# Input differences inside the delta rule's last steps, the gate weights read first, and a set of transposes spread over three steps

## What is computed

```python
h = rms_norm(x, norm_pre[i])
(aq, ak, av, az, dq, dk, dv, db, da, dz, gate_att, gate_dn) = split_cols(h @ w_in[i])
...
o_dn = bidir_gated_deltanet(qd, kd, vd, g, beta).astype(x.dtype)
o_dn = rms_norm(o_dn.transpose(0, 2, 1, 3), dn_norm[i]).reshape(B, S, DN_VW)
y_dn = (o_dn * jax.nn.silu(dz)) @ w_br_dn[i]
mix = (jax.nn.sigmoid(gate_att) * y_att + jax.nn.sigmoid(gate_dn) * y_dn) @ w_out[i]
```

```python
v_new = u_c - jnp.einsum('bhcd,bhdv->bhcv', w_c, state)
o = (jnp.einsum('bhcd,bhdv->bhcv', q_c * jnp.exp(g_c)[..., None], state)
     + jnp.einsum('bhcj,bhjv->bhcv', a_c, v_new))
k_dec = k_c * jnp.exp(g_last[..., None] - g_c)[..., None]
state = state * jnp.exp(g_last)[..., None, None] + jnp.einsum('bhcd,bhcv->bhdv', k_dec, v_new)
```

## Time and profile before

| what | value |
|---|---|
| median of 3 runs | 1669.21 us (1666.99 to 1671.65) |
| profiled execution, its own time | 1670.91 us |
| profiled execution, span in the trace | 1669.1 us |
| granted TensorE clock, mean | 0.959 |
| PE busy | 1478.6 us, 89% |
| DVE busy | 675.9 us, 40% |
| ACT busy | 380.5 us, 23% |
| POOL busy | 296.7 us, 18% |

### The profile page before, as it was taken

One profiled execution on the slowest core, in us unless ns is written; L12 is line 12 of the kernel. 1 busy time (PEld: TensorE's weight loads), 2 busy tenths in 40 slices (PEclk: granted clock), 3 DMA queues, 4 the chain that ended last, 5 costly groups with the idle time before them and its releaser, 6 DMA issues. The chain is left out here.

```text
span 1669.1 us, 22426 instructions
## 1 busy us (share of the span) xinstructions
PE 1478.6 (89%) x8686; PEld 995.7 (60%) x8686; DVE 675.9 (40%) x1203; ACT 380.5 (23%) x814; POOL 296.7 (18%) x261
## 2 busy tenths in 40 slices
PE   5998998999999978988999999999988968887782
PEld 5864445884544457777888778674657854332320
DVE  3321435124369956775232154310363444332224
ACT  3213445104333333321110132301231010000001
POOL 0020011620007244563540000000000002111110
PEclk9999999999999979999999999999988978999996
DMA  6128210213112213434322030322133066999994
GB/s 208 49 81 261 68 51 26 84 43 126 51 51 76 64 64 126 130 131 136 101 86 92 1 126 26 78 64 79 38 93 127 1 241 238 422 425 425 424 388 170
DMA packets 118385, 228.27 MB, mean 137 GB/s; under 512 B 13202, under 2 KB 102896, under 8 KB 109332
## 3 DMA queue, kind: packets, MB, share of 16 engines
q1 hardware_dynamic: 112963, 216.34, 36.0%
q0 software_dynamic: 5184, 8.55, 1.4%
q10 hardware_dynamic: 144, 2.10, 0.3%
HBM read 221.56 MB, written 15.74 MB: 142 GB/s over the span
## 5 line engine op out<-in xcount | busy, mean ns | idle before, releaser
L917 PE MATMUL psv<-arena 128*128 128x256 f32 x800 | 175.8, 379 | 2.7 <-ACT arena L1681 1.3
L882 PE MATMUL psv<-arena,wslot 128*128 128x512 f32 x384 | 170.8, 598 | 1.8 <-DVEq L2154 1.8
L917 PEld LDWEIGHTS psv<-arena 128*128 128x128 f32 x800 | 151.6, 190 | 25.3 <-issue 4.9
L1586 ACT ACTIVATE arena<-pss 128x512 f32<-128x512 f32 (+1 forms) x157 | 84.8, 540 | 333.1 <-PE pss L882 275.2
L882 PE MATMUL pss<-wslot,arena 128*128 128x256 f32 (+1 forms) x640 | 147.6, 391 | 4.6 <-issue 2.0
L882 PE MATMUL pss<-arena 128*128 128x256 f32 (+1 forms) x512 | 141.7, 434 | 6.3 <-ACTq L151 3.1
L1504 PE MATMUL pss<-arena 128*64 128x512 f32 x384 | 123.9, 655 | 18.8 <-DMA arena<-w_expert_in 16.4
L882 PEld LDWEIGHTS pss<-wslot,arena 128*128 128x128 f32 x640 | 120.7, 190 | 30.3 <-issue 11.8
L882 PEld LDWEIGHTS pss<-arena 128*128 128x128 f32 x512 | 95.9, 190 | 45.6 <-issue 29.8
L882 PEld LDWEIGHTS psv<-arena,wslot 128*128 128x128 f32 x384 | 71.1, 190 | 85.5 <-issue 83.0
L2364 DVE SCALAR_TENSOR_TENSOR arena<-psv,ccols,arena 128x510 f32<-128x510 f32 (+1 forms) x96 | 71.9, 749 | 59.9 <-ACT arena L1737 56.8
(11 more groups left out here) (339 smaller groups left out, 1977.6 us busy)
## 6 DMA issues: line engine op xcount, KB each, us to landing
arena<-w_expert_in SPq DMA_DIRECT2D x24, 2048.0 KB, 18.3
wslot<-w_in SPq DMA_DIRECT2D x32, 1024.0 KB, 5.4
arena<-w_expert_out SPq DMA_DIRECT2D x32, 1024.0 KB, 18.8
wslot<-w_ada SPq DMA_DIRECT2D x18, 1024.0 KB, 5.2
wslot<-w_expert_in SPq DMA_DIRECT2D x8, 2048.0 KB, 16.0
arena<-w_in SPq DMA_DIRECT2D x10, 1024.0 KB, 8.7
arena<-w_ada SPq DMA_DIRECT2D x6, 1024.0 KB, 7.9
arena<-x SPq DMA_DIRECT2D x8, 512.0 KB, 8.6
```

The source lines that it names most:

```text
L882: m = mm(o, l, r, start=(n == 0), stop=(n == len(pairs) - 1))
L917: m = mm(o[:, j * HALF_T:(j + 1) * HALF_T], l[:, c, j * P:(j + 1) * P], r[:, c, :], start=new and j == 0 and c == 0, stop=j == 1 and c == ...
L1586: L.did(A(dst, src, func, **kw), s[sig] if sig else None, [s["free_s"]])
```

## The change

Four edits are made together.

1. POOL makes the input differences `terms(hT, term_z, n)` for the `dz` and `gd` products behind its work in loop passes n = 4 (one), 5 (two) and 6 (one) of the delta rule, where before they followed `phase(3)`. They lie in the parts of `vtok` that are no longer read.
2. `last_part(4)` also moves ahead of `phase(3)`. Its output has a place of its own (`part_z`), and the held parts `held_b` move.
3. SP issues `dz` 2 and 3 first after `phase(3)`, then `gd` 0 and 1, and only then the parked `mixT`; norm rows, x, p and ctx follow between later weights, since `pin` and `ctxt` now share memory with the differences.
4. The transposes for g = 1 are spread: one half in step 0, two in step 1, one and the multiply in step 2, each ahead of the state update. `turn_back` has an argument for the halves.

```diff
@@ SP
             sp.wait_ge(s["phase"], 4 * 3)
+            stream_to(("gd", 1))
             load(mixT.rearrange("p c n -> p (c n)"), mix_dram.rearrange("(p n) -> p n", p=P), "mix_kept")
+            stream_to(("gd", 3))
             load(rowv, a["norm_post"].partition_broadcast(P), "ld_res")
             load(rowv2, a["ple_norm"].partition_broadcast(P), "ld_res")
             for t in range(NT):
                 load(x1[:, t, :], a["x"][0, t * P:(t + 1) * P, :], "ld_res")
+            stream_to(("brd", 1))
+
+            sp.wait_ge(s["full_v"], SEVEN_JOB[4] + 2)
             load(pin, a["p"][0, 0].rearrange("(t p) n -> p t n", p=P), "ld_p")
+            stream_to(("brd", 3))
+
+            sp.wait_ge(s["full_v"], SEVEN_JOB[8])
@@ POOL
+                if n == 4:
+                    terms(hT, term_z, 0)
+                if n == 5:
+                    terms(hT, term_z, 1)
+                    terms(hT, term_z, 2)
+                if n == 6:
+                    terms(hT, term_z, 3)
+            parts(4, part_z)
+            last_part(4, part_z)
             phase(3)
-            for n in range(3):
-                terms(hT, term_z, n)
-            last_part(4, part_b)
-            terms(hT, term_z, 3)
             for u in range(5, 7):
                 parts(u, part_b)
                 last_part(u, part_b)
@@ DVE
                 if n == 0:
                     dve.wait_ge(s["bsub_ready"], 1)
-                    turn_back(1, True)
+                    turn_back(1, True, (0,))
+                if n == 1:
+                    turn_back(1, True, (1,))
+                    turn_back(1, False, (0,))
+                if n == 2:
+                    turn_back(1, False, (1,))
+                    L.raise_(s["bt_ready"])
...
-                if n == 1:
-                    turn_back(1, False)
-                    L.raise_(s["bt_ready"])
```

More of the change, by code:

```diff
@@ L321, in build @@
         part_b = [at(tt_at, 4, WC), at(tt_at + 4 * K, 4, WC), at(B + 108 * K, 4, WC)]
[L322 to L325, removed]
+        part_z = part_b[0:2] + [at(B + 48 * K, 4, WC)]
+        held_b = [at(B + 96 * K + n * SEQ, 2, HALF_T) for n in range(4)]
+        term_z = [at(B + 60 * K, 4, HALF_T), at(B + 56 * K, 4, HALF_T), hT[:, 0:4, HALF_T:SEQ],
+                  at(B + 52 * K, 4, HALF_T)]
         term_n = [at(B + 64 * K, 4, HALF_T), at(B + 68 * K, 4, HALF_T), onT[:, 0:4, HALF_T:SEQ],
@@ L1228, in _ @@
             phase(3)
-            seven(4, hT, part_b, term_z, True)
+            seven(4, hT, part_z, term_z, True)
             for t in range(NT):
@@ L2069, in _ @@
                         keys(n + 1, hg)
-            parts(4, part_b)
+                if n == 4:
[7 more added lines that the diff above has]
+            last_part(4, part_z)
             phase(3)
-            for n in range(3):
-                terms(hT, term_z, n)
-            last_part(4, part_b)
-            terms(hT, term_z, 3)
             for u in range(5, 7):
@@ L2310, in inverse_norms, with turn_back @@
                     scale(o, o, c1, s["rk_in"])
-            def turn_back(g, first):
-                for x in range(2):
+            def turn_back(g, first, halves=(0, 1)):
+                for x in halves:
                     X = inv_X[HX[x], g, :, :]
@@ L2318, in turn_back @@
                                       X.rearrange("p r c -> p c r") if flip else X))
-                if not first:
+                if not first and 1 in halves:
                     mul(TTb[:, g], TT32[:, g], spread(co_b[:, g * 32:(g + 1) * 32], 32))
```

## The result

The changed kernel is slower: median 1678.13 us (1675.46 to 1679.69, 5 executions) against 1670.4 for the kernel before (5 executions on the same chip), a ratio of 1.0056 with the interval 1.0045 to 1.0068. A second comparison gave 1.0057 (1.0040 to 1.0074). One execution of a later kernel, `e6_last_part_behind`, took 3926.6 us and is left out of its ratio. The forecast was 1671, no change that can be told, with a range up to 1676: both are wrong.

The account below looks back on a forecast made before the run. PE, busy 89%, was taken to bound the kernel. Terms -4.3 + 1.0 + 4.8 + 0 = +1.5 us on the profiled 1670.91 give 1672.4; with the median 1.7 lower, the forecast was 1671, range 1663.5 to 1676.

Parts of the forecast that it names:

- Transposes: Delta rule steps 1 and 2: without DVE's transposes and multiply between them, step 2 shortens; -4.3 us, bounds -4.7 and -1.0.
- Differences in the steps: Passes 4 to 6: PE waits 2.5 to 2.9 us for POOL's key decay, costing 0.2 to 1.4 us.
- The last part ahead of phase(3): POOL's last part reaches DVE's last output additions, one of which may wait: 0 to 1 us on arrival at T, `phase(3)`.
- Behind phase(3): `seven(4)`: POOL's `parts(5)` and last part collide with DVE's four multiplies, delaying PE's last half; +4.8 us, bounds -2.1 and +4.8.
- The clock: Last half of `seven(4)`: low clock behind the wait both before and after; 0 more, bounds -1.7 and +3.7 us.
- rival 2: Last half of `seven(4)` and transposes behind it: 8 us wait holds PE at 1.2 GHz, +3.7, total 1674.4 us; chance 0.16.
- Reordered transfers: Behind `phase(3)`: `mixT`, x, p and ctx come later but are used only from `seven(8)`, over 80 us on; 0 us.
- The sum: Whole kernel: -4.3 + 1.0 + 4.8 + 0 = +1.5 us on the profiled execution, forecast median 1671.
- Rival 1: Behind `phase(3)`: DVE's multiplies don't collide with POOL; 1662 us, or 1664 if the clock still falls; chance 0.19.

Follow-up runs that it names:

- e6_last_part_behind: Changed kernel with `parts(5)` held until DVE's multiplies are done, one difference per pass 3 to 6, last part behind `phase(3)`: 1664.89 us, 0.9966; again 1663.71, 0.9974.
- after_again: The changed kernel itself, run a second time: 1679.58 us, ratio 1.0057 to the kernel before.
- e7: Changed kernel with only the last part of `seven(4)` moved back behind `phase(3)`: 1673.4 us, ratio 1.0030 to the kernel before.
- p1: Changed kernel with 2 repeated matmuls (0.9 us) ahead of the first product with `w_out`: ratio 1.0057 to the kernel before.
- p2: Changed kernel with 4 repeated matmuls (1.7 us) ahead of the first product with `w_out`: ratio 1.0068 to the kernel before.
- p3: Kernel before with 6 repeated matmuls (2.6 us) ahead of the first product with `w_out`: ratio 1.0013 to the kernel before.
- e1: Kernel before with the spread transposes alone: 1665.21 us, ratio 0.9972; again 1666.2 us, 0.9981.
- e5: Kernel before with only the new order of transfers (`dz` 2 and 3 and `gd` ahead of `mixT`, x, p, ctx): 1673.59 us, ratio 1.0029.
- e2: Changed kernel with POOL's `parts(5)` held until DVE's four multiplies are done: 1667.65 us, ratio 0.9994 to the kernel before.

## Why the prediction was wrong

**Transposes: right.** Steps 1 and 2 together are 3.9 us shorter in the trace (+0.30 and -4.24), forecast 4.3; alone they are worth 3 to 5 us.

**Differences in the steps: the wait right, its cost too high.** 2.62 us on PE as forecast. `phase(3)` is 4.4 us earlier, forecast 3.3. From step 6's start to step 7's new values the change costs 0.3 us (21.13 against 20.81), at the low end of the forecast's 0.2 to 1.4; the wait before the new values shrank so far that they kept their clock, 2.0 us that I had not counted (from them to the inner output 4.27 against 6.30). In after_again they did not keep it (3.44 us behind 3.17 us of waiting). A slip without effect: the forecast's terms for the key decay add up to 715.9 to 716.2, not to 716.2 to 716.6.

**The last part ahead of phase(3): the first step that failed.** "One of which may wait for POOL, 0 to 1 us." The addition did wait, 1.2 us. But I priced only the arrival at T, and not that PE's wait ahead of T grows from 1.75 to 2.94 us, behind which the next half runs at low clock for a while (+1.5). I had the rows for that: 2.12 us had been enough before the last half. The term was 0 to 1 us and is 2.7 in the trace; by the ratios of e7 and e6 it is 2.5 to 4.7.

**Behind phase(3): mechanism right, the clock missing from the term.** Forecast +4.8, measured +6.9 (43.01 - 36.12). The last half begins at T+31.35, forecast 30.4: 1.5 of that is the slow first half, and without it, in e7, it is T+29.86. So the collision itself costs 4.2 us (29.86 - 25.66), a little less than forecast, and the low clock 1.5 in the first half and 1.2 in the last. The multiplies take 11.22 us, forecast "some 11".

**The clock: the second step that failed.** "I take 0 more, bounds -1.7 and +3.7." The last half takes 6.57 us, 1.2 more than before, behind 7.83 us of waiting. This is rival 2's mechanism at a third of its price. Summed over the execution the low clock accounts for more than these 2.7 us (mean 0.957 against 0.961). The sum had no term for what lies behind `seven(5)`, and 3 to 7 of the 9.4 us are there: at 775 us the two traces of the changed kernel are 2.5 and 6.3 us behind (3.3 of the 6.3 already at the start of step 2). Over four traces each (p1, p2 and p3 count too, since their added work comes later) the changed kernel reaches `seven(5)` at 775.5 us on the mean and the kernel before at 772.4, which leaves some 6 of the 9.4 us behind it. Reckoned so for the others (their traces for the start of `seven(5)`, their ratios for the total), every kernel built on the changed one loses 2 to 6 us behind it, and those built on the kernel before (e1, e5, p3) lie between a gain of 1.4 and a loss of 3.1. That points at something which all of the first have, moved buffers among it, but one trace against a median is a rough measure, and no run takes it apart. The traces put this rest behind 1160 us, at waits that every kernel has; why the changed kernel pays more there on the mean stays open.

The Trainium skill, "SBUF — State Buffer", section "Who interferes with whom", has it that a DVE instruction with two SBUF inputs and a GpSimd instruction that reads SBUF exclude each other. The multiplies agree, with a small second input too: 2.0 to 2.1 us for each POOL instruction, which takes 2.35 alone. Both sides lose: of POOL's three that met them, one took 2.35 us and two 3.2. Work of 5.00 and 3 x 2.35 us, one after the other, would take 12.05; from 750.59 to 761.83 it took 11.24, so the exclusion is near whole in these rows, not quite.

**Reordered transfers: right as far as seen.** 0 was forecast, and between 775 and 1160 us nothing was lost. e5, with edit 3's order alone, is 5 us slower, and the collision with its clock makes 6.1 of its stage.

**The sum.** In the first trace up to `seven(5)` it is +2.5, forecast +1.5: only 1 us off, by errors of both signs, which is luck. By the ratio it is +9.4, and the forecast had nothing for what the low clock costs elsewhere. Rival 1 (no collision, 1662 or 1664) was built as e2, and that is 1667.65: taking the collision away gave back 10 us, but the last part's price and the rest behind 1160 us stayed. Only with the last part moved too, in e6, was it 1663.7 to 1664.9.

## What to carry to other kernels

A load brought forward is also a release: look up which engine starts on it and what it will lie beside. Here one wait on an engine that nobody waited for turned a loss of 9 us into none. When an edit lengthens a wait of PE by a microsecond, price what follows the wait at both clocks, not only the wait. A trace that ends its sum at the changed stage says nothing of the rest: compare landmarks down to the end, in more than one trace of each kernel. And work moved ahead of a meeting point of all engines should be checked against the last thing that each of them does there.

## What the runs showed of the hardware

DVE beside POOL, float32: the four multiplies of 128x1024 take 5.00 us alone and 7.02, 9.19 and 11.22 us with one, two and three POOL instructions of 128x1024 on them. Which inputs DVE's instruction has matters: inside POOL's last part (727.19 to 729.87 in the changed kernel) an addition of 128x512 with one input in PSUM took its usual 0.69 us (at 727.69), and the next, with both in SBUF, 1.88.

The wait ahead of the stage's first half and the half itself, over nineteen traces: behind 1.72 to 2.01 us of waiting it took 3.72 us in all eleven, behind 2.72 to 3.19 it took 5.12 to 5.41 in all seven (p1, behind 2.57, took 3.72). But the length of a wait does not decide alone: behind 2.12 us before the last half, the three traces of the kernel before show 5.34 to 5.38 us for the same half size and both of e1 3.69, and behind 2.3 to 2.7 us of waiting for a weight at 1165 us the same 64 matmuls took 14.08 us in some traces and 15.6 to 15.8 in others, of the same kernel too. Executions of one kernel scatter by 8 us (1664.0 to 1671.9 in 30 of the kernel before), so one profile is no measure of a total, and the profiled execution of e5 was 6.7 us above its median.
